# The modulation of a two-layer decoder step split in two: 4 of its 24 panels before the input projection, 20 between its tiles, which go by token quarters

## The reference, cut to what matters

```python
def modulation(c, w_mod, b_mod):
    m = jax.nn.silu(c) @ w_mod + b_mod            # w_mod[l]: 1024 x 6144, l = 0, 1
    return [q[:, None, :] for q in jnp.split(m, 6, axis=-1)]
...
sh_m, sc_m, g_m, sh_f, sc_f, g_f = modulation(c, p['w_mod'][l], p['b_mod'][l])
h = rmsnorm(x, p['norm_mix_pre'][l]) * (1 + sc_m) + sh_m
...
proj = h @ w_in                                   # 1024 x 2208
gate_out, gate_in, xa, cq, ckv, kpe = jnp.split(proj, ...)
z_hist = jnp.concatenate([conv_hist, gate_in * xa], axis=1)
ya = gate_out * causal_dwconv(z_hist, conv_w)
q = (rmsnorm(cq, q_norm) @ w_q_up).reshape(b, s, N_HEADS_B, NOPE_DIM + ROPE_DIM)
ckv = rmsnorm(ckv, kv_norm)                       # output new_cache_ckv
kpe = apply_rope(kpe, cos, sin)                   # output new_cache_kpe
```

## Time and profile before

| | |
|---|---|
| median of 3 runs | 3592.28 us |
| the profiled execution | 3588.77 us |
| its span | 3587.0 us |
| TensorE busy | 3165.3 us (88%) |
| VectorE busy | 1626.9 us (45%) |
| ScalarE busy | 1056.0 us (29%) |
| GpSimd busy | 953.5 us (27%) |
| mean granted TensorE clock | 0.941 |

### The profile page before, as it was taken

How to read it: one execution, slowest core, us unless ns; L and a number is a source line. 1 busy time by engine, 2 the same in 40 slices (tenths; PEclk the granted TensorE clock), 3 DMA queues, 4 the chain that set the end, 5 groups by cost and what they waited for, 6 DMA issues and landing times. The chain is left out here.

```text
span 3587.0 us, 60727 instructions
## 1 busy us (share of the span) xinstructions
PE 3165.3 (88%) x24253; PEld 2841.9 (79%) x24253; DVE 1626.9 (45%) x2817; ACT 1056.0 (29%) x1810; POOL 953.5 (27%) x602
## 2 busy tenths in 40 slices
PE   5849979989999788999999996695288999999998
PEld 3439947666666488999999995695188999999997
DVE  5743134534444345343334338499536333333335
ACT  4631113634444344211111125210334211111113
POOL 0022205743333153212211214220353211221112
PEclk9969979989999899999999998897699999999999
DMA  8921110025555332211111102110132211111112
GB/s 296 328 80 41 36 43 1 1 95 174 169 164 170 96 96 80 60 41 47 47 41 41 47 25 81 59 41 10 29 104 69 66 47 35 53 41 47 35 36 94
DMA packets 237248, 274.87 MB, mean 77 GB/s; under 512 B 12082, under 2 KB 185003, under 8 KB 236964
## 3 DMA queue, kind: packets, MB, share of 16 engines
q1 hardware_dynamic: 216108, 197.31, 17.7%
q0 software_dynamic: 20992, 75.51, 6.5%
HBM read 248.89 MB, written 24.26 MB: 76 GB/s over the span
## 5 line engine op out<-in xcount | busy, mean ns | idle before, releaser
L948 PE MATMUL ps<-HS,w_split 128*128 128x272 f32 x9600 | 1235.4, 291 | 61.9 <-POOL w_split L1306 61.9
L948 PEld LDWEIGHTS ps<-HS,w_split 128*128 128x128 f32 x9600 | 1226.1, 191 | 65.6 <-POOL w_split L1306 50.2
L1306 POOL TENSOR_TENSOR w_split<-w_raw,w_split 128x1024 fp32r<-128x1024 f32 x144 | 344.4, 2400 | 1226.9 <-ACT w_split L1056 1226.9
L956 PE MATMUL ps<-hid,w_split 128*128 128x272 f32 x4224 | 554.3, 291 | 3.1 <-DVE hid L1489 2.9
L956 PEld LDWEIGHTS ps<-hid,w_split 128*128 128x128 f32 x4224 | 540.4, 190 | 8.3 <-DVE hid L1489 3.4
L1558 DVE TENSOR_TENSOR Y<-Y,ps 128x272 f32<-128x272 f32 x576 | 252.3, 438 | 175.9 <-PE ps L956 175.9
L1056 ACT ACTIVATE w_split<-w_raw 128x1024 fp32r<-128x1024 f32 x144 | 148.8, 1050 | 504.5 <-PE ps L956 448.3
L1480 DVE TENSOR_TENSOR sg<-sg,ps 128x272 f32<-128x272 f32 x176 | 76.4, 437 | 391.5 <-ACT sg L1141 391.5
L695 PE MATMUL ps<-HS_in,w_split 128*128 128x272 f32 x1728 | 218.9, 289 | 37.3 <-POOL w_split L672 37.3
L695 PEld LDWEIGHTS ps<-HS_in,w_split 128*128 128x128 f32 x1728 | 218.7, 190 | 38.1 <-issue 38.1
L695 PE MATMUL ps<-HS,w_split 128*128 128x272 f32 x1536 | 194.5, 289 | 23.1 <-POOL w_split L672 23.1
(11 more groups left out here) (329 smaller groups left out, 3678.5 us busy)
## 6 DMA issues: line engine op xcount, KB each, us to landing
w_mod<-w_mod_in SPq DMA_DIRECT2D x24, 2048.0 KB, 8.9
w_raw<-w_ffn_gate_in SPq DMA_DIRECT2D x44, 512.0 KB
w_raw<-w_ffn_up_in SPq DMA_DIRECT2D x44, 512.0 KB, 3.9
w_raw<-w_ffn_down_in SPq DMA_DIRECT2D x44, 512.0 KB, 3.6
x_part<-x_spill SPq DMA_DIRECT2D x64, 272.0 KB, 3.0
x_spill<-Y SPq DMA_DIRECT2D x12, 1088.0 KB, 5.5
w_raw<-w_in_ab_in SPq DMA_DIRECT2D x18, 512.0 KB, 3.9
w_raw<-w_in_cd_in SPq DMA_DIRECT2D x16, 512.0 KB, 3.9
```

What stands on the lines that cost most here:

```text
L948: ins = pe.matmul(bank(b), wt[:, a, k, :], HS[:, e, k, qs(q)], start=(k == 0 and j == 0), stop=(k == KD - 1 and j == 2))
L956: ins = pe.matmul(bank(b), slots[1 + f][:, a, d * P:(d + 1) * P], hid[:, e, f, qs(q)], start=(f == 0 and j == 0), stop=(f == 1 and j == 2))
L1306: pool.tensor_tensor(slots[slot][:, 1, :], raw[u][:, :], slots[slot][:, 0, :].bitcast(F32), ALU.subtract).then_inc(w_lo, 1)
```

## The change

The five stages become two.

`stage_begin` loads x, the first two tiles of w_in and the first two panels of w_mod on ScalarE's DMA queue, beside the constants on SP's. ScalarE and VectorE take turns in copying turned x. The squares are summed by full matmuls with ones, the first two weight tiles are split, and the first 4 panels are multiplied. Panels are no longer split: the product takes plain fp32, and `panel_products` puts four of the 8 feature blocks on four column groups of 32, in two rounds; the result is turned and its four parts are added by VectorE (`tensor_reduce`). The third and fourth panel lie in x's buffer, and are loaded when it has been turned. Five of x's eight blocks are stored to `x_spill` here.

`stage_front` does the rest. It makes h by quarters, in four small buffers (VectorE the row scale, ScalarE twice scale and shift, GpSimd the low part), a quarter ahead of the products. A unit is 24 matmuls of one tile and one quarter; there are 72. The first 16 units take four tiles (cq 0 to 2, ckv 0) quarter by quarter, the other 14 tiles (ckv 1, kpe, then gates and xa) follow in turn. Five PSUM banks go around; one serves sums, swap and tokens, and two serve the panels. Before the units of `p_at` (4, 8, ..., 72, and 42 and 58) a whole panel is multiplied, 20 in all, from two half buffers of 1024 KB; one unit later it is turned. Sums of squares, rotary steps and the turning and storing of ckv and kpe stand between units too. SP's list is sorted by the unit to which a job belongs.

TensorE's list, in the modulation before: the 16 products of a panel, and the 4 short ones that fold and turn another.

The diff, cut to its core:

```diff
-        with ExitStack() as cond:
-            c.cT = tile(nc, cond, "cT", [P, KD, 9], side="right")
-            stage_setup(c)
-            stage_modulation(c, c.Y)
-        stage_norms(c, c.Y, HS, pre=(0, M_SCM, M_SHM), spill=spill)
...
-            stage_ab_in(c, HS, ya, cq, ckv, kq)
-                stage_ab_norms(c, ya, cq, ckv, kq, cos, sin, ctok)
-                stage_attention(c, cq, ckv, kq, cos, sin, yb, qlat, qpe)
+                stage_begin(c, c.Y, spill)
+                tab = tile(nc, tables, "rope", [P, T], side="right")
+                HS = tile(nc, fr, "HS_in", [P, 2, KD, T], F32R, side="right")
+                stage_front(c, HS, ya, cq, ckv, kq, tab, ctok, spill)
+            stage_attention(c, cq, ckv, kq, tab, yb, qlat, qpe)
...
+MW = 512
+NPANEL = 2 * 6 * D // MW
+NFIRST = 4
+CP = 32
+def panel_products(pe, c, bank, panel, k0, start, stop):
+    for kk in range(4):
+        ins = pe.matmul(c.ps[CP * kk:CP * kk + CP, bank, :], c.cpad[:, k0 + kk, :], panel[:, kk, :], start=start, stop=stop,
+                        skip_group_check=True)
+    return ins
+def stage_begin(c, X, spill):
...
+            x_done(sp, XT)
+            sp.dma_start(spill[:, KS:KD, :], X[:, KS:KD, :]).then_inc(x_out, 16)
...
+                if t in (XH, XT):
+                    u = NFIRST // 2 + t // XH - 1
+                    act.dma_start(panel[u], w_cols(c.w_mod[0], u * MW, MW)).then_inc(p_in[u], 16)
...
+            for k in range(KD):
+                pe.wait_ge(squared, k + 1)
+                for q in range(4):
+                    ins = pe.matmul(c.ps[:, q, 0:Q], c.ones[:, :], sq[k % 2][:, q * Q:(q + 1) * Q], start=(k == 0),
+                                    stop=(k == KD - 1))
+                ins.then_inc(summed, 1)
+            for i in range(NFIRST):
+                panel_sum(i)
+                turn_panel(i)
...
+def stage_front(c, HS, ya, cq, ckv, kq, tab, ctok, spill):
+    NSL, NBK = 4, 5
+    N = 4 * NFT
+    units = [(t, q) for q in range(4) for t in range(NSL)] + [(t, q) for t in range(NSL, NFT) for q in range(4)]
+    p_at = sorted([4 * (i + 1) for i in range(N // 4)] + [42, 58])
+    hi_after = {4: 12, 5: 13, 6: 14, 7: 15} | {t: 4 * t - 13 for t in range(8, NFT)}
+    turn_at = {p + 1: i for i, p in enumerate(p_at)}
...
+            def load(t):
+                if t >= 4:
+                    sp.wait_ge(w_lo, t - 3)
+                sp.dma_start(raw[t % 2][:, :].rearrange("p (k n) -> p k n", k=KD), w_cols(w_d, front_column(t))
+                             ).then_inc(w_in[t % 2], 16)
+            def load_panel(h):
+                if h >= 2:
+                    sp.wait_ge(p_half, h - 1)
+                sp.dma_start(pan[h % 2][:, :, :], src).then_inc(pan_in[h % 2], 16)
...
+            jobs = [(-3.0 + t / 10, load, t) for t in range(2, 6)]
+            jobs += [(hi_after[t - 2] + 0.6, load, t) for t in range(6, NFT)]
+            jobs += [(-2.0 + h / 10 if h < 2 else p_at[h // 2 - 1] + 0.5 + h % 2 / 10, load_panel, h) for h in range(2 * NPL)]
+            jobs += [(n + 0.9, store_tokens, t) for n, t in token_at.items()]
...
+                if n < 16:
+                    pe.wait_ge(h_lo, 8 * (q + 1) + (1 if q == 3 else 0))
...
+            for n in range(N + 2):
+                if n in sum_at:
+                    sum_squares(sum_at[n])
+                if n in swap_at:
+                    swap(swap_at[n])
+                if n in token_at:
+                    turn_tokens(token_at[n])
+                if n in turn_at:
+                    turn_panel(turn_at[n])
+                if n in p_at:
+                    panel(p_at.index(n))
+                if n < N:
+                    product(n)
```

More of the change, by code:

```diff
@@ L1646, in _, with scale_parts @@
                         copy_out(dve, t)
-def stage_ab_in(c, HS, ya, cq, ckv, kq):
+def scale_parts(dve, c, l, parts):
+    for part, row, one in ((M_SCM, R_MIXPRE, True), (M_GM, R_MIXPOST, False), (M_SCF, R_FFNPRE, True),
+                           (M_GF, R_FFNPOST, False)):
+        if part in parts:
+            g = c.par[:, 1, row + 8 * l:row + 8 * l + 8].unsqueeze(2).broadcast_to([P, KD, 9])
+            m = c.mod[:, NM * l + part:NM * l + part + KD, :]
+            if one:
+                dve.scalar_tensor_tensor(out=m, in0=m, scalar=1.0, in1=g, op0=ALU.add, op1=ALU.mult)
+            else:
+                dve.tensor_tensor(m, m, g, ALU.mult)
@@ new lines, in stage_begin @@
+        page_row = tile(nc, cm, "page_row", [P, 2, NB])
+        XT = NPR // P
+        x_nat = tile(nc, cm, "x_nat", [P, XT, D])
+        xs_nat = tile(nc, cm, "xs_nat", [NSA, D])
+        panel = [tile(nc, cm, f"w_mod{u}", [P, KD, MW])[:, :, :] for u in range(NFIRST // 2)]
+        panel += [x_nat[:, u * XT // 2:(u + 1) * XT // 2, :].rearrange("p t (h n) -> p (t h) n", n=MW)
+                  for u in range(NFIRST // 2)]
+        sq = [tile(nc, cm, f"squares{u}", [P, T]) for u in range(2)]
+        part = tile(nc, cm, "mod_part", [P, MW // P, 9])
@@ new lines, in _ @@
+            for n in range(N + 2):
[11 more added lines that the diff above has]
+                    product(n)
+            pe.wait_ge(last_set, KA)
@@ L1722, in _, with high @@
[L1722 to L1728 removed]
+            def high(q, k):
+                n = Q if q < 3 else QP
+                act.wait_ge(h_made, 8 * q + k + 1)
+                t, bias, scale = hr[k % 4][:, 0:n], c.mod[:, M_SHM + k, 0:1], c.mod[:, M_SCM + k, 0:1]
+                act.activation(HS[:, 0, k, q * Q:q * Q + n], t, ACT.Identity, bias=bias, scale=scale)
+                act.activation(t, t, ACT.Identity, bias=bias, scale=scale).then_inc(h_hi, 1)
@@ new lines, in _ @@
+            for k in range(KD):
+                high(0, k)
+            to_hi(2)
+            to_hi(3)
+            for n in range(N + 2):
+                if n in sum_at:
+                    root(sum_at[n])
+                if n in token_at:
+                    copy_tokens(token_at[n])
+                if n in p_at:
+                    copy_panel(p_at.index(n))
+                if n < N:
+                    t, q = units[n]
+                    if n < 12:
+                        high(q + 1, 2 * t)
+                        high(q + 1, 2 * t + 1)
+                    if n == 11:
+                        act.wait_ge(s_step, 3)
+                        act.activation(HS[:, 0, :, NPR:T], hs, ACT.Copy).then_inc(h_hi, 1)
+                    if by_act[n]:
+                        empty(n)
+                    for t in range(4, NFT):
+                        if hi_after[t] == n:
+                            to_hi(t)
```

1069 lines of the change are left out of this document (505 added, 564 removed).

## The result

The changed kernel took 3474.85 us (median of 4 runs, 3473.03 to 3478.04), the kernel before on the same chip 3592.73 us. The ratio is 0.9676, 95% interval [0.966, 0.9693]: faster by 118 us. Forecast was 3467 us with a range of 3434 to 3530. The profiled execution took 3478.04 us, its span is 3476.3 us, its mean clock 0.949.

The account below looks back on a forecast made before the run. It took w_mod's transfer to bound the modulation, 5.78 us a panel. `stage_begin` and TensorE's list in `stage_front` put attention's start at 378 instead of 501.35 us, 123 us less than 3588.77: 3465.5, forecast 3467 us, range 3434 to 3530.

Parts of the forecast that it names:

- `stage_begin`, 63 us: First stage: TensorE's chain of turning, sums and four panels ends later than the transfer's 52 us; bounds 54 to 72 us.
- the part on hidden work: In `stage_front`: work of ScalarE, GpSimd, VectorE and DMA issuing (about 0.5 us each) costed at nothing, as hidden by the units.
- the sums: Sums of squares in `stage_begin`: 32 fp32 matmuls take 14.6 us, with 2 us more while the clock is at 1.2 GHz.
- The first h, 9.6 us: Start of `stage_front`: ScalarE's activations 7.7 us, plus VectorE's first, GpSimd's last and hand-overs, before the first products.
- 72 units at 3.04 us: TensorE's large products in `stage_front` take 219.0 us, as before, slow start included.
- A panel, 2.7 us: TensorE's cost per panel in `stage_front`: products 1.72, turning 0.46, shape changes 0.5 us; 20 panels 53 us.
- changes of shape: Changes between wide and narrow matmuls around each panel: bounded by 0 and 0.5 us each, half taken, twice a panel.
- Waits for panels and the clock behind them, 18 us: In `stage_front`: 14 us of TensorE waiting for panels, 5 at the first and 4 at unit 42, plus 4 us clock lost.
- Behind attention's start, nothing: The stages from attention's first DMA on keep their length; only their start moves, from 501.35 to 378 us.
- late panels: Rival for `stage_front`: slower transfers or SP held longer make every panel late, adding 80 us, 3547 us; chance 0.11.
- Groups in series: Rival for panel products: column groups do not run side by side, 6.9 instead of 1.72 us, 3591 us; chance 0.05.
- The clock: Rival for the front: narrow work between units drops TensorE to 1.2 GHz, adding 262 us, 3729 us; chance 0.04.

Follow-up runs that it names:

- e6: The kernel before with 6 of its 24 panels computed, the rest of the modulation a constant; 3483.41 us beside 3584.81 for the kernel before.
- e1: The changed kernel with the first two weight tiles and first two panels issued from SP's queue in place of ScalarE's; 3461.81 us.
- e5: The changed kernel without the 20 panels of `stage_front`, the later modulation a constant; 3418.61 us.
- e3: The changed kernel with SP's list reordered: first panel ahead of tiles 4, 5 and the spill; from tile 8 on, tile loads behind the panel's halves; 3465.64 us.
- e2: The changed kernel with all eight products of a panel on one column group, one after the other; 3579.86 us.
- e7: The changed kernel with the edits of e1 and e3 together, and the sums of squares also in four column groups; 3444.56 us.
- e8: e7 with 32 one-column memsets of an unused tile added to VectorE's list in `stage_begin`; 3452.55 us.
- e9: e7 with 96 one-column memsets of an unused tile added to VectorE's list in `stage_begin`; 3446.13 us.

## Why the prediction was right, and where it was not

The forecast was 7.85 us, 0.2%, below the time. It took the right bound on each side: w_mod's transfer before (5.78 us a panel, e6: 5.6), TensorE's own list after. That it came so near is in part luck, since a first stage forecast too short and a front forecast too long offset each other. Its terms:

- **`stage_begin`, 63 us: measured 76.7.** This is the term that was mis-sized, and its failed step is the last sentence of the part on hidden work: "The DMAs on ScalarE's queue cost it about 0.5 us each in issuing". That came from the row of two x loads at an empty queue. The two panels, behind 5.4 MB issued before them, held ScalarE for 17.8 us, and the turning of x waited for its sigmoid. e1 undid just this and `stage_begin` ended at 63.10 us, the forecast's number. The bounds for the stage were 54 to 72, so even these were too narrow: both were built from the transfer and from TensorE, and none from the engine that issues. The kernel before gave no such price: there SP issued a panel in 0.40 us right behind x. The other steps of this stage held: the sums 17.4 us for 16.6, a panel 3.2 us from start to start for 3.0.
- **The first h, 9.6 us: 9.9.**
- **72 units at 3.04 us:** in the piece read above 12.28 us for four, 3.07 each, with a panel and a turning among them, and 3.02 in the undisturbed row of e5.
- **A panel, 2.7 us: 2.3.** From its start to the next unit's 1.85 us for 1.72, the turning 0.35 for 0.46; of the 0.5 us for changes of shape about half was there. The Trainium skill ("TensorEngine Tiling (Array Packing)", Key Properties) has the engine drained at a change of tiling mode. In this kernel each panel is two such changes. The 2.32 us hold 1.72 of products and 0.35 of turning, if the products' estimate is right, which leaves 0.25 us; beside e5's 3.02 us a unit instead of 3.04 it is 0.33. So by the trace all that a panel's changes of shape cost, a drain included, is 0.25 to 0.33 us. A gap of 0.76 us as in the earlier trace rows, from which I took the bound, does not fit twice into that; what it was isn't shown.
- **Waits for panels and the clock behind them, 18 us: 12.9 us at the two large places**, 6.8 at unit 4 and 6.0 at unit 42, the low clock included (forecast 5 and 4, and 4 more for the clock); no other wait was over 0.7 us. e3 gave 11.7 us back. Of the two causes named, SP's place in line for tile 15 and the first panel's behind the spill, e3 moved both at once, so their shares weren't tested apart.
- **Behind attention's start, nothing: +4.5 us between the two profiled executions.** 3588.77 - 115.27 = 3473.5 us, and the profiled execution took 3478.04. 3.3 us of it are VectorE's late addition, which e6 shows without the change. The whole part behind attention's start takes 3085.7 us of the span in the kernel before, 3090.2 in the changed one, 3085.3 in e1 and 3087.3 in e6. So the 4.5 us lie within what executions differ by, and no cost of the change can be read from them; one profile of the kernel before can't rule out a small one. Between the medians the gain is 117.9 us, against 115.3 at attention's start.

The prediction's line "That is 304 us, up to 376.5 us" has a slip: its items add up to 299.9 us, and to 372.5. The unrounded sum behind it uses the items themselves and is right. The forecast is 13.7 us too little in the first stage, 5.6 too much in the front, 4.5 too little behind, and 3467 was 1.5 over the unrounded 3465.5: 12.6 - 1.5 = 11.1 us, which is 3478.04 - 3467; the median lies 3.2 under the profiled run.

The rivals: late panels did not come (the waits cost 12.9 us, not 80). Groups in series would have been e2, 3580 us, as priced within 11 us (3591). The clock stayed at 0.97 in the front, notwithstanding: long waits came twice there and not between all units. The Trainium skill ("TensorE: Matmul & The Clock Gate", "A second HAM failure mode: psum-queue depth-cycling") tells of a kernel in which it swings with the small pauses between groups of matmuls; the front has small groups between almost all its units and does not swing. The trace shows the low level only behind waits for DMA or for another engine, as in the windows of 0.72 and 0.62 and in e7's of 0.50.

## What to carry to other kernels

When a stream whose transfer is the bound can be laid between large products, its price becomes what TensorE spends on it; here 5.6 us a panel became 3.0, but only since narrow products ran in four column groups. An engine with work to do should not issue the large early DMAs: an issue at an empty queue gives no price for one behind others, so look in the profile for how long the issuer is held, and move the issues to an engine for which nothing waits. In one queue, a load that waits for another engine belongs behind loads whose buffer is already free. The best version, e7, is 30 us under the changed kernel by the edits of e1 and e3 and the grouped sums.

## What the runs showed that I had not expected

- Issuing can hold the issuer: 17.77 us for two 2048 KB transfers on ScalarE's queue behind others of its own, 8.38 us for two 512 KB ones on SP's in e1, against 1.04 us for the two at the start. In e1 ScalarE issued 2048 KB in 0.37 us while SP was held, so it is not the core's whole traffic that holds.
- Eight fp32 matmuls of 512 columns with 32 stationary columns take 1.92 us on four column groups and 7.05 us on one.
- A reciprocal on VectorE of 272 elements a partition took 1.85 us in e7, e8 and e9, one of 1088 elements 6.95 us in the changed kernel.
- At the start of the gathers VectorE began an addition 2.1 to 5.5 us after the products it needs had ended, in twelve profiles of thirteen.
